# Two network blocks on one core: a new order for the scan, for the first loads and for the layer norm seams

## What is computed

```python
zxbcdt = x @ w_in                       # z | xbc | dt
xbc = silu(causal_conv(xbc) + conv_b)   # xs (64 heads of 64), B, C (8 groups of 128)
dt = softplus(dt_raw + dt_bias)
y = ssd_chunked(xs, dt, -exp(a_log), B, C) + xs * d_skip
y = group_rms(y * silu(z)) * norm_w
x = layernorm(ALPHA * x + y @ w_out)    # first seam; k, v, q, gate follow
h = sliding_window_attention(x, k, v) * silu(gate)
x = layernorm(ALPHA * x + h @ b_out)    # second seam; second block follows
x = x + neighbourhood_attention(rms_norm(x)) @ w_o
x = x + relu(rms_norm(x) @ w1) ** 2 @ w2
```

## Time and profile before

| | us |
|---|---|
| median of 3 runs | 2163.44 |
| lowest and highest | 2161.64, 2164.19 |
| the profiled execution | 2161.41 |
| its span, first to last instruction | 2159.4 |
| PE busy in the span | 2134.1 (99%) |
| DVE busy | 1361.0 (63%) |
| ACT busy | 1082.6 (50%) |

### The profile page before, as it was taken

The page is one execution under the profiler, slowest core; times in us unless marked ns, Lnnn a source line. Parts: engine busy times, 40 slices in busy tenths (PEclk is TensorE's granted clock), DMA queues, the critical chain, the costliest instruction groups (busy, mean ns, idle before and its releaser), DMA issues.

```text
span 2159.4 us, 32571 instructions
## 1 busy us (share of the span) xinstructions
PE 2134.1 (99%) x12154; PEld 1851.9 (86%) x12154; DVE 1361.0 (63%) x1668; ACT 1082.6 (50%) x1418; POOL 130.3 (6%) x142
## 2 busy tenths in 40 slices
PE   8999999999999999999999999999999999999999
PEld 8988889999888778998788888888888888888887
DVE  6777776777545668765777665555655645555554
ACT  4544457877333455673444555454434434443442
POOL 2000001111000100000024300000000000000000
PEclk9999999999999999999999999999999999999999
DMA  7577765665666654457576554556556666656664
GB/s 238 183 204 206 215 200 168 180 188 167 225 194 196 201 182 140 155 177 217 170 216 197 166 156 137 164 168 196 191 194 189 188 194 193 187 193 194 188 191 160
DMA packets 207158, 403.02 MB, mean 187 GB/s; under 512 B 16228, under 2 KB 18404, under 8 KB 206772
## 3 DMA queue, kind: packets, MB, share of 16 engines
q1 hardware_dynamic: 199168, 385.92, 57.3%
q0 software_dynamic: 4192, 14.50, 3.0%
q10 hardware_dynamic: 3668, 0.73, 0.2%
HBM read 395.27 MB, written 5.83 MB: 186 GB/s over the span
## 4 chain that ended last, share of the span: by engine, by line
PE 95%; DVE 3%; ACT 1%; issue 1%; DMA 0%; POOL 0%; DVEq 0%; ACTq 0%
PE ps L413 16%; PE ps L415 16%; PE ps L414 16%; PE ps L394 14%; PE ps L399 7%; PE ps L381 6%; PE ps L382 6%; PE ps L383 6%; DVE xbc L1614 1%; PE ps L1181 1%; DVE wlo L368 1%; PE ps L1364 1%; PE ps L1387 1%; PE ps L1480 1%; PE ps L1454 1%
## 5 line engine op out<-in xcount | busy, mean ns | idle before, releaser
L368 DVE TENSOR_TENSOR wlo<-raw,whi 128x1024 fp32r<-128x1024 f32 x712 | 873.9, 1233 | 714.9 <-ACT whi L363 711.4
L363 ACT ACTIVATE whi<-raw 128x1024 fp32r<-128x1024 f32 x712 | 753.8, 1060 | 1010.4 <-PE ps L415 568.0
L394 PE MATMUL ps<-xhl,whi 128*128 128x512 f32 x1472 | 369.4, 393 | 0.6 <-issue 0.2
L381 PE MATMUL ps<-xhl,whi 128*128 128x256 f32 x1088 | 315.6, 290 | 9.7 <-DVE wlo L368 9.7
L382 PE MATMUL ps<-xhl,whi 128*128 128x256 f32 x1088 | 309.0, 284 | 0.0
L383 PE MATMUL ps<-xhl,wlo 128*128 128x256 f32 x1088 | 308.9, 284 | 0.0
L394 PEld LDWEIGHTS ps<-xhl,whi 128*128 128x128 f32 x1472 | 265.0, 189 | 49.5 <-DVE wlo L368 1.6
L413 PE MATMUL ps<-whi,xhl 128*128 128x512 f32 x760 | 303.8, 400 | 2.0 <-DVE xhl L1867 2.0
L415 PE MATMUL ps<-whi,xhl 128*128 128x512 f32 x760 | 296.5, 390 | 0.0
L414 PE MATMUL ps<-wlo,xhl 128*128 128x512 f32 x760 | 296.4, 390 | 0.0
L381 PEld LDWEIGHTS ps<-xhl,whi 128*128 128x128 f32 x1088 | 209.7, 193 | 12.1 <-issue 12.1
(11 more groups left out here) (252 smaller groups left out, 2052.9 us busy)
## 6 DMA issues: line engine op xcount, KB each, us to landing
raw<-w SPq DMA_DIRECT2D x256, 512.0 KB, 4.3
raw<-w_in SPq DMA_DIRECT2D x160, 512.0 KB, 4.4
raw<-w_qkv SPq DMA_DIRECT2D x96, 512.0 KB, 3.9
raw<-w_out SPq DMA_DIRECT2D x64, 512.0 KB, 4.5
raw<-b_in SPq DMA_DIRECT2D x64, 512.0 KB, 3.7
raw<-b_out SPq DMA_DIRECT2D x32, 512.0 KB, 4.3
raw<-w_o SPq DMA_DIRECT2D x32, 512.0 KB, 3.8
cumb<-cum_scratch SPq DMA_DIRECT2D x16, 512.0 KB, 4.4
```

Of the source, the lines that this page charges most:

```text
L363: act.activation(whi[:, u % RING], raw[:, u % RING], ACT.Copy).then_inc(S("hi_ready"), 1)
L368: dve.tensor_tensor(wlo[:, u % RING], raw[:, u % RING], whi[:, u % RING].bitcast(F32), ALU.subtract).then_inc(S("lo_ready"), 1)
L381: pe.matmul(o, w_h, ah[:, k, :], start=(k == 0 and n % 2 == 0), stop=False, skip_group_check=True)
L394: pe.matmul(ps[:, bank + n, :], whi[:, u % RING, t, n * P:(n + 1) * P], both, start=(k == 0), stop=False, skip_group_check=True)
```

## The change

Five things are altered.

1. In group 0, DVE writes the third and the fourth scan matrix in slot 6, behind the reads of pairs 0 and 1 and in front of that slot's split.
2. `xT` comes in eight pieces of 256 KB, each in front of its unit, and ACT and DVE split piece and unit in turn for all eight.
3. Of the eleven later small loads ACT keeps `wdt` (behind `whi` of unit 4); the other ten go to POOL, which waits for the last piece of x first. The `rel_bias` loads stand behind them.
4. PE multiplies the identity 36 times (`WARM`) before unit 0, as soon as `ident` is there.
5. At both seams three units are held in place of two; one weight split and the first `xhat` piece stand between the two halves of `last_rows`; the first step of `scaled` hands over its two tiles one by one, and PE's first unit waits for each half of its input by itself.

```diff
-WEIGHTED_AT, FIRST_WEIGHTED_AT = (1, 2, 5, 6), (0, 2, 6, 7)
+WEIGHTED_AT, FIRST_WEIGHTED_AT = (1, 2, 5, 6), (0, 2)
+TAIL = 3
-SMALL = 14
+FIRST, SMALL = 4, 10
+WARM = 36
...
             for t in range(2):
+                if halves:
+                    pe.wait_ge(S(halves[t][0]), halves[t][1])
...
-            pe.wait_ge(S("lo_ready"), u + 2)
+            pe.wait_ge(S("lo_ready"), u + TAIL)
             for m in range(TT):
-                for e in range(2):
+                for e in range(TAIL):
...
-                if c < RING:
-                    sp.dma_start(xin[:, 4 * c:4 * c + 4, :], xv[:, 4 * c:4 * c + 4, :]).then_inc(S(f"x_in{c}"), 16)
+                sp.dma_start(xin[:, 2 * c:2 * c + 2, :], xv[:, 2 * c:2 * c + 2, :]).then_inc(S(f"x_in{c}"), 16)
                 load_unit(sp, c, 0, v[c][:, :, 2 * INNER:2 * INNER + PANEL])
...
+            pool.wait_ge(S(f"x_in{UPP - 1}"), 16)
+            small_loads(pool, "small_in")(small[3:-1])
+            g.wait(pool, z)
+            for n in range(DIAGS):
+                pool.dma_start(padrow[...], rel_bias[...]).then_inc(S("pad_in"), 16)
             pool.wait_ge(S("cum_ready"), 1)
...
-            for c in range(4):
+            for c in range(UPP):
                 act.wait_ge(S(f"x_in{c}"), 16)
-                act.activation(xh[:, 4 * c:4 * c + 4, :], ...)
+                act.activation(xh[:, 2 * c:2 * c + 2, :], ...)
                 split_hi(act, c, 0)
-            load_small(small[3:])
-            for c in range(RING):
-                split_hi(act, RING + c, 0)
+                if c == RING:
+                    load_small(small[-1:])
             act.wait_ge(S("const_ready"), 1)
+            act.wait_ge(S("first_in"), 16 * FIRST)
             act.wait_ge(S("small_in"), 16 * SMALL)
...
+            pe.wait_ge(S("ident_ready"), 1)
+            for _ in range(WARM):
+                pe.transpose(ps[:, 7, 0:P], ident[:], ident[:])
             acc_free(0, 0)
             for c in range(UPP):
-                pe.wait_ge(S("xl_ready"), c // 2 + 1)
+                pe.wait_ge(S("xl_ready"), c + 1)
...
                     if j in m_at and j < 5 and (g > 0 or j > 0):
                         weighted(PAIRS * g + m_at.index(j))
+                    if g == 0 and j == FIRST_Y_AT[0] + 1:
+                        weighted(2)
+                        weighted(3)
...
                     residual(D // PANEL - 1, m, par)
                     norm_stats(m)
+                    if m == 0:
+                        split_lo(dve, end - TAIL + RING, 0)
+                        xhat(n, 0, 0)
...
+                if kp == 0:
+                    for n, sem in enumerate(("x_first", "x_ready")):
+                        dve.wait_ge(S("xtmp_first"), 2 * (first // UPP) + n + 1)
+                        hi, lo = xh[:, n, :], xl[:, n, :]
+                        s = d.done(dve.tensor_copy(hi, xtmp[:, 0, n]))
+                        d.wait(dve, s)
+                        dve.tensor_tensor(lo, xtmp[:, 0, n], hi.bitcast(F32), ALU.subtract).then_inc(S(sem), 1)
+                    return
...
-                for m, at in ((0, 0), (0, 1), (1, 0), (1, 1), (0, 2), (1, 2)):
+                for m, at in ((0, 1), (1, 0), (1, 1), (0, 2), (1, 2)):
```

More of the change, by code:

```diff
@@ L450, in wait, with small_loads, load @@
                 eng.wait_ge(S(name), value)
+        small = ((cw[:], conv_w), (cb[:], conv_b), (nw[:], norm_w), (d2[:], d_skip), (dtb[:], dt_bias),
+                 (alog[:], a_log), (gcol[:], ln_gc), (bcol[:], ln_bc), (rcol[:], gains),
+                 (qg[:], q_gain), (kg[:], k_gain), (posi[:], pos),
+                 (snk[:], sinks.rearrange("(a n) -> a n", a=1).to_broadcast([P, AH])),
+                 (wdt[:], w_in[:, INNER + CONV_DIM:INNER + CONV_DIM + SSM_HEADS].rearrange(
+                     "(k p) n -> p k n", p=P)))
+        def small_loads(eng, sem):
+            def load(some):
+                for dst, src in some:
+                    eng.dma_start(dst, src).then_inc(S(sem), 16)
+            return load
         block = es.enter_context(nc.Block())
@@ L533, in _ @@
             z = g.done(pool.memset(padrow[:], 0.0))
-            g.wait(pool, z)
-            for n in range(DIAGS):
-                pool.dma_start(padrow[n * NH:(n + 1) * NH, GW - WW:GW - WW + BW], rel_bias[:, WH - ROWS + n, :])\
-                    .then_inc(S("pad_in"), 16)
             g.wait(pool, a)
@@ L845, in scaled @@
                                           bias=shift[:, k:k + 1], scale=gain[:, k:k + 1])
-                last.then_inc(S("xtmp_ready"), 1)
+                    if kp == 0:
+                        last.then_inc(S("xtmp_first"), 1)
+                if kp > 0:
+                    last.then_inc(S("xtmp_ready"), 1)
             def entry_panel(first, prod, gain, shift):
@@ L1257, in out_pair @@
                         pe.wait_ge(S("yl_ready"), c // 2 + 1)
-                        if last and par == 1 and c >= 2 * UPP - 2:
-                            if c == 2 * UPP - 2:
-                                token_tail(pe, OUT + D // PANEL * 2 * UPP - 2, c, 2 * par, yh, yl, XS_TILES)
+                        if last and par == 1 and c >= 2 * UPP - TAIL:
+                            if c == 2 * UPP - TAIL:
+                                token_tail(pe, OUT + D // PANEL * 2 * UPP - TAIL, c, 2 * par, yh, yl, XS_TILES)
                             continue
@@ L1329, in entry_panel @@
                 for c in range(UPP):
-                    pe.wait_ge(S("x_ready"), UPP * prod + c + 1)
-                    token_unit(pe, first + c, 0, c, 2 * par, xh, xl, KT)
+                    ready = ("x_ready", UPP * prod + c + 1)
+                    token_unit(pe, first + c, 0, c, 2 * par, xh, xl, KT,
+                               halves=(ready if c else ("x_first", prod // 2 + 1), ready))
                     if c + 4 < UPP:
@@ L1596, in _ @@
             dve.tensor_copy(dcol[:], ps[:, 7, 0:XS_TILES])
[L1598 removed]
+            dve.wait_ge(S("xl_ready"), UPP)
             one = d.done(dve.memset(dv["one"][:], 1.0))
@@ L1808, in out_panel @@
             def out_panel(i, par, first, last=False):
-                for c in range(2 * UPP - 2 if last else 2 * UPP):
+                for c in range(2 * UPP - TAIL if last else 2 * UPP):
                     split_lo(dve, OUT + RING + 2 * UPP * par + c, i * 4)
@@ L1833, in out_panel, with xhat @@
                     residual(i * 2 + par, m, par)
+            def xhat(n, m, at):
+                if at == 0:
+                    dve.wait_ge(S("rstd_ready"), TT * n + m + 1)
+                v = xtok[:, m, at * PANEL:(at + 1) * PANEL]
+                last = dve.tensor_scalar(v, v, mv[:, m, 0:1], rstd[:, m:m + 1], ALU.subtract, ALU.mult)
+                if m == TT - 1:
+                    last.then_inc(S("xhat_ready"), 1)
             def last_rows(n, end, par):
@@ L1850, in _ @@
             last_rows(0, KV, 1)
[L1852 to L1863 removed]
+            def scaled(prod, kp, first):
+                if kp == 0:
+                    for n, sem in enumerate(("x_first", "x_ready")):
[5 more added lines that the diff above has]
+                    return
+                dve.wait_ge(S("xtmp_ready"), (UPP - 1) * (first // UPP) + kp)
                 hi, lo = xh[:, 2 * kp:2 * kp + 2, :], xl[:, 2 * kp:2 * kp + 2, :]
@@ L2026, in wo_panel @@
                 if split:
-                    for c in range(UPP - 2 if last else UPP):
+                    for c in range(UPP - TAIL if last else UPP):
                         split_lo(dve, WO + RING + s_ * UPP + c, i * 2)
```

37 lines of the change are left out of this document (10 added, 27 removed).

## The result

The changed kernel takes 2150.89 us (median of 5 runs, 2150.68 to 2151.29), the kernel before 2162.89 on the same chip (5 runs, 2161.64 to 2164.19). The ratio is 0.9945, 95% interval 0.9931 to 0.996: faster by 0.55%. The profiled execution took 2150.89 as well, with a span of 2149.2: 10.5 us less in time and 10.2 less in span than the profiled execution before.

The account below looks back on a forecast made before the run. PE, busy 99% of the span, bounds the kernel; only its idle time and slow-clock products can shrink. 6.4 + 2.8 + 2.0 = 11.2 us off the 2163.4 median gives 2152.2, stated as 2152.0; forecast range 2150.0 to 2154.0, eight in ten 2149.8 to 2157.5.

Parts of the forecast that it names:

- Scan: Group 0, pairs 2 and 3: early matrices give back 5.5 us of waiting and 0.9 of slow clock, 6.4 together.
- Rival C: Scan's wait only moves to pairs 4 and 5 of group 1; up to 5.5 of 6.4 us given back; chance 0.08.
- Start: Ahead of and in unit 0: earlier data gain 1.3 us, identity products take over 1.5 of slow running; 2.8 in all.
- Rival A: At the start, identity products end late; takes 2.3 or up to 3.8 us off the gain; chance 0.12.
- Small loads: Ten loads moved from ACT to POOL, landing at 29 to 31; taken as 0, with up to 3 us lost.
- the far end of the loss: Small loads at `dcol`: 26 + 8.7 + 2.5 = 37.2 less 32.2, a loss of 5.0 us at most.
- Rival D: POOL's issues of the small loads so slow that the kernel is slower; 3 us each gives 2169; chance 0.02.
- Seams: Two seams between row stages: PE restarts 0.85 us earlier, plus 0.15 from `rstd`; 1.0 each, 2.0 together.
- the third held unit gives nothing: At the seams, the third held unit alone gains 0, since DVE is not late; up to 0.3 us lost allowed.

Follow-up runs that it names:

- two_held: Changed kernel with two held units at both seams instead of three and no weight split between the row halves; 2151.73 us.
- scan_undone: Changed kernel with the third and fourth scan matrices of group 0 back behind the splits of slots 6 and 7; 2157.69 us.
- no_warm: Changed kernel without the 36 identity products ahead of unit 0; 2152.54 us.
- four_pieces: Changed kernel with x loaded and split in four pieces of 512 KB again, each in front of every second unit; 2150.67 us.
- halves: Changed kernel with ACT's and DVE's splits of units 0 and 1 in two halves, PE waiting for each, and 26 identity products; 2149.86 us.
- early_ident: Changed kernel with units 0 and 1 split in halves, the identity built first on GpSimd, and 28 identity products; 2149.11 us.
- whole: Changed kernel with the first step of the scaled rows handed over whole again at both seams; 2152.01 us.
- third_only: Changed kernel with only the third scan matrix early and the fourth back behind the split of slot 7; 2153.8 us.
- bias_first: Changed kernel with POOL's seven rel_bias loads in front of its ten small loads; 2154.18 us.
- dve_shift: Changed kernel with two small clears of an unused tile, with a wait each, at the head of VectorE's program; 2150.22 us.

## Why the prediction was right

**Scan: 6.4 forecast, 6.3 by position, 6.2 by undoing it.** Both halves of the term stand: the wait, and the products behind it at the lower clock. Rival C (a new wait in group 1) did not come; no wait for a matrix is left in the whole trace.

**Start: 2.8 forecast, 2.86 measured.** Its two terms were 1.3 and 1.5. Without the identity products PE starts at 8.07, and undoing them costs 1.4. The earlier data give 1.35 (9.71 less 8.36), but for a reason that the prediction had only in part: it gave all of it to the smaller piece, and some 0.4 is the move of the `rel_bias` loads, which took POOL's selects away from DVE's first split. The faster unit 0 gives 4.46 - 2.95 = 1.51. The two together are 2.86, and that this is also the total is luck, as two parts that the prediction put at nothing cancel: the hold by the identity products took 0.24, and the stall ahead of unit 4 in the kernel before gave 0.24 back. The prediction had put ACT's issues at 0, as hidden under four ready units; they were hidden but for this stall. The identity products ran slowly for 4.4 us, not for the 3.3 of the sum. Rival A was partly true: the identity products, not the data, released unit 0, which cost 0.24 us in the profiled execution and up to 0.84 in others (two_held, where the split was done at 7.93 and unit 0 began at 8.91).

**Small loads: 0 forecast, 0 measured, by 0.6 us.** POOL's first issue was at 20.70 (19 to 21 forecast), the last one ended at 26.42 (24 to 26) and the loads had landed by 29.20 (29 to 31). From there ACT's 1.06 and DVE's 1.23 lead to 31.53. The price of a landing was read too widely: the 4.7 to 8.7 of the earlier trace rows also counts seven later stores from `padrow` (issued from 109 us on). The seven loads alone landed 4.7 to 5.3 us after their issue. With 5.3 the far end of the loss, 5.0 in the prediction, is 26 + 5.3 + 2.5 - 32.2 = 1.6; the forecast used the lower end and does not change. By the fixed cost of about 2 us that the Trainium skill gives ("DMA: Bandwidth & Descriptors", section "Anatomy of one DMA — SWDGE (gpsimd) path") it would have been 28.4; the row shows 2.8 behind the last issue, between that and the 4.7 taken from the full stream. The slowing of descriptor writes by VectorE, for which the prediction named the same page, did not show: an issue took 0.52 to 0.59, and 0.78 once, up to 24.2 while DVE worked with short breaks, and 0.55 behind that, where DVE idled. (Rival D's sum does not come out either: at 3 us for each of ten issues instead of 2 the kernel would be 10 us slower than before, not 6. Nothing else rests on it.)

**Seams: 1.0 each forecast, 0.91 and 0.92 measured.** Mostly the half hand-over, 0.76 by undoing it, where 0.85 was forecast; the 0.15 that is left fits POOL's quicker `rstd`, as forecast. The sentence that the third held unit gives nothing left out what it covers: the early piece, 0.47 per seam.

**The sum was 11.2, the span shows 10.2.** Of what is missing 0.25 is at the seams and in the scan; the rest is in no step: 0.3 in the wide panel, where the new pause of DVE holds PE up by 0.44, 0.35 in the last store, 0.16 between. The start gave 0.06 back. Against the median it came out the other way: the medians differ by 12.0, since the profiled execution of the kernel before, 2161.41, was faster than each of the five timed ones, and since the time outside the span fell from 2.0 to 1.7. The profiled time forecast, 2150.2, was 0.7 too low, the median forecast, 2152.0, 1.1 too high. Both gaps are within the 2.6 us over which the kernel before itself varies.

**Open.** Why the kernel before spreads over 2.6 us and the changed one over 0.6. A part lies outside the span: in 29 further executions of the kernel before, timed beside the experiments, it was 2.0 to 2.4 us in 20 and 3.0 to 4.0 in nine, while it was 1.7 in the changed kernel; the cause is not known. For the spread within the span, a start and a long pause, each followed by slow running of varying length, would do it, but that is argued from the spread of scan_undone and no_warm (1.0 and 0.9), not shown.

## What to carry to other kernels

A wait that is fed by a chain through two other engines is removed by moving all the links in front of the one that waits for PE, not only the first; price it with the products behind it, which may run at the lower clock. Products that only keep the clock up should start as early as possible and be few enough to end, at the slow distance, before the data come: none at all cost 1.4 us here, a pause of 0.8 or 1.2 between their end and the data did not bring the clock down, and each one too many costs its whole length. Reserve behind moved loads was 0.6 us here; before moving anything onto a software queue, count what stands ahead of it and what the engine that waits has left. Read the price of a load from a view that holds that load alone.

## What the runs showed of the hardware

**The rise of the clock varies between executions.** Four traces, at the stretch in which the identity products change from 0.21 to 0.11 apart. The count in the first brackets is PE's, of all products that run in some part of the half us: 4 or 5 when they are slow, 7 when they are fast. The changed kernel, four_pieces, halves, early_ident:

```profile
6.50:7.00 0.50, 0.50 (x4) 0.50 (x3) 1.00 0.95 356
7.00:7.50 0.50, 0.50 (x7) 0.50 (x6) 1.00 1.08 340
```

```profile
5.00:5.50 0.50, 0.50 (x4) 0.50 (x3) 1.00 1.08 389
5.50:6.00 0.50, 0.50 (x7) 0.50 (x6) 1.00 1.07 382
```

```profile
7.00:7.50 0.50, 0.50 (x4) 0.50 (x3) 1.00 1.05 377
```

```profile
4.00:4.50 0.50, 0.50 (x4) 0.50 (x4) 1.00 1.06 414
4.50:5.00 0.50, 0.50 (x6) 0.50 (x5) 1.00 1.06 408
```

The products started at 2.55 in the first three and at 1.60 in the last, so the slow stretch lasted 4.4, 2.9, over 4.9 and about 3 us. These are four kernels, but whole and two_held, whose start is the changed kernel's, vary as much, with some 3 and over 4.9. In early_ident the rise, at about 4.6, came before that of every trace in which PE began at 2.55 (5.4 at the earliest): it went with PE's own start, in this one trace, and not with the time since the program began. The granted clock is 1.00 in all these rows; at the start of the program it does not tell the level, the distance of the products does. The Trainium skill ("TensorE: Matmul & The Clock Gate", "Part 1: The HAM clock gate") says that the number of slow products at a kernel's start changes from run to run; the traces agree.

**Not every pause drops the clock.** In the traces it stayed at the 2.4 GHz level behind 2.54 (third_only) and 1.20 us (four_pieces), fell to 0.56 behind 4.66 (scan_undone), and fell to 0.52 behind 1.93 (bias_first), where a nearly empty stretch of two small products stood just ahead; no run shows whether that made the difference. The times of the other runs suggest that at some 2 us it varies between executions of one kernel: two of five runs of third_only took 0.9 more, one of four of bias_first 1.6 less.

**A pause in VectorE's program**, 0.52 us where it is 0.15 in other versions, at one place, went away when two instructions were added 170 us earlier (dve_shift).
